# Two products instead of one transpose: x's transpose updated level by level in the RWKV recurrence of a long fused kernel

## What is computed

```python
def step(s, inp):
    r_t, w_t, k_t, v_t, a_t, b_t = inp
    sa = jnp.einsum('bhvk,bhk->bhv', s, a_t)
    s = s * w_t[:, :, None, :] + sa[..., :, None] * b_t[:, :, None, :] + v_t[..., :, None] * k_t[:, :, None, :]
    return s, jnp.einsum('bhvk,bhk->bhv', s, r_t)
...
for d, (rev, s0) in enumerate(((False, s0_f), (True, s0_b))):
    ...
    y, s = wkv_scan(s0, r, decay, kd, v, -kk, kk * a, rev)
    y_sum = y_sum + y
```

## Time and profile before

| | us |
|---|---|
| median of 3 runs | 2635.47 (2632.21 to 2637.56) |
| the profiled execution, its time | 2638.92 |
| its span in the trace | 2637.1 |
| busy in the span: TensorE, VectorE, ScalarE, GpSimd | 2322.0, 1605.5, 1076.4, 661.7 |
| the recurrence, first to last TensorE record | 1380.8 to 1813.1 |

### The profile page before, as it was taken

One profiled execution on the slowest core, in us unless ns is written; L12 is line 12 of the kernel. 1 busy time (PEld: TensorE's weight loads), 2 busy tenths in 40 slices (PEclk: granted clock), 3 DMA queues, 4 the chain that ended last, 5 costly groups with the idle time before them and its releaser, 6 DMA issues. The chain is left out here.

```text
span 2637.1 us, 50916 instructions
## 1 busy us (share of the span) xinstructions
PE 2322.0 (88%) x21292; PEld 1828.3 (69%) x21292; DVE 1605.5 (61%) x1953; ACT 1076.4 (41%) x1833; POOL 661.7 (25%) x659
## 2 busy tenths in 40 slices
PE   5998988799989579999768999999982999999993
PEld 3876755468868468888527778887661888888883
DVE  5981559541124455566484444443657999999994
ACT  3112541321014410000245655554240877777773
POOL 1221668113310023222015655550000000000000
PEclk8998999999999689999679999998995999999997
DMA  6332014511113445211161111103233999999994
GB/s 234 112 112 66 1 57 130 159 59 48 52 67 145 146 154 196 75 41 33 39 217 39 28 28 28 28 20 123 76 145 119 389 407 395 395 403 398 394 380 157
DMA packets 136488, 401.83 MB, mean 152 GB/s; under 512 B 56314, under 2 KB 67834, under 8 KB 108754
## 3 DMA queue, kind: packets, MB, share of 16 engines
q1 hardware_dynamic: 124180, 360.02, 36.8%
q0 software_dynamic: 4608, 16.78, 2.6%
q10 hardware_dynamic: 7488, 21.99, 2.2%
HBM read 341.05 MB, written 57.69 MB: 151 GB/s over the span
## 5 line engine op out<-in xcount | busy, mean ns | idle before, releaser
L3895 DVE TENSOR_TENSOR ex_wl<-ew_raw,ex_wh 128x2048 fp32r<-128x2048 f32 x192 | 435.6, 2290 | 42.2 <-ACT ex_wh L3857 38.1
L3857 ACT ACTIVATE ex_wh<-ew_raw 128x2048 fp32r<-128x2048 f32 x192 | 367.6, 1920 | 108.4 <-PE ex_U L3801 40.3
L118 PE MATMUL sp_acc<-b2h_hi,sp_wh 128*128 128x512 f32 (+1 forms) x528 | 194.9, 369 | 16.8 <-POOL sp_wl L1729 16.8
L118 PE MATMUL sp_acc<-b2h_lo,sp_wh 128*128 128x512 f32 (+1 forms) x528 | 194.7, 369 | 0.0
L118 PE MATMUL sp_acc<-b2h_hi,sp_wl 128*128 128x512 f32 (+1 forms) x528 | 194.4, 368 | 0.0
L3778 POOL DMA_INDIRECT x<-ex_o,ex_at x16 | 26.5, 1657 | 494.6 <-DVE ex_o L3918 494.6
L2512 DVE COPY_PREDICATED rc_x<-b_level,rc_chain 128x256 f32<-128x256 uint32 x160 | 64.1, 444 | 132.2 <-PE rc_chain L2600 131.6
L1727 POOL CAST sp_wh<-sp_w 128x1024 fp32r<-128x1024 f32 x26 | 28.9, 1111 | 402.5 <-DMA sp_w<-in_w_conv 226.5
L118 PEld LDWEIGHTS sp_acc<-b2h_hi,sp_wh 128*128 128x128 f32 x528 | 100.2, 190 | 34.6 <-POOL sp_wl L1729 17.2
L118 PEld LDWEIGHTS sp_acc<-b2h_hi,sp_wl 128*128 128x128 f32 x528 | 100.1, 190 | 16.6
L118 PEld LDWEIGHTS sp_acc<-b2h_lo,sp_wh 128*128 128x128 f32 x528 | 100.2, 190 | 16.3
(11 more groups left out here) (520 smaller groups left out, 5986.7 us busy)
## 6 DMA issues: line engine op xcount, KB each, us to landing
ew_raw<-in_exp_gate SPq DMA_DIRECT2D x64, 1024.0 KB, 7.5
ew_raw<-in_exp_up SPq DMA_DIRECT2D x64, 1024.0 KB, 9.3
ew_raw<-in_exp_down SPq DMA_DIRECT2D x64, 1024.0 KB, 7.9
b2p_pT<-in_ada_w SPq DMA_DIRECT2D x32, 512.0 KB, 6.0
rc_ac<-ac SPq DMA_DIRECT2D x40, 256.0 KB, 3.7
b_pj<-in_ada_w SPq DMA_DIRECT2D x8, 1024.0 KB, 12.1
ssm_wm<-in_w_merge SPq DMA_DIRECT2D x16, 512.0 KB
ac<-rp_ac SPq DMA_DIRECT2D x4, 2048.0 KB, 7.1
```

Source lines behind the costliest of these rows:

```text
L118: ins = nc.tensor.matmul(out, w[a][:, k, :], h[b][:, k, cols], start=(first and n == 0), stop=(last and n == 2))
L3857: nc.scalar.activation(wh[:, n % RING], raw[:, n % RING], ACT.Copy).then_inc(q["w_hi"], 1)
L3895: V.tensor_tensor(wl[:, n % RING], raw[:, n % RING], wh[:, n % RING].bitcast(f32), ALU.subtract).then_inc(q["w_lo"], 1)
```

## The change

From the second level on x is no longer transposed. `turned_x` for a level l of 1 to 4 now computes, with `staying`, the transposed update t1 against xt of the level before, and a new step `turned` on VectorE copies the new blocks into xt by COPY_PREDICATED, as `inverse` did already behind the last level. The first level's transpose and its copy on ScalarE stay. `factored` of levels 1 to 4 now also waits until the new product has read the old t1. The orders of TensorE, ScalarE, VectorE and GpSimd are written anew.

```diff
@@ ScalarE
 def factored(c, d, l):
     if runs(c):
         act.wait_ge(q[d]["t1_done"], LEVELS * c + l + 1)
+        if l:
+            act.wait_ge(joint["xt_done"], LEVELS * c + l + 1)
         A.activation(paired(t[d]["t1"][:]), chained(d), ACT.Copy, scale=-1.0).then_inc(q[d]["t1_ready"], 1)
...
 def v_rows(c, d, e):
...
         act.wait_ge(joint["v_done"], c + 1)
+        if c:
+            act.wait_ge(joint["s_done"], c)
+        if c > CTX_CK:
+            act.wait_ge(joint["y_crossed"], c - CTX_CK)
@@ ScalarE's order
-                    transposed(k - 2, 1, 1)
-                    transposed(k - 2, 0, 1)
...
@@ VectorE
+def turned(c, d, l):
+    if runs(c):
+        b, s = t[d], q[d]
+        dve.wait_ge(joint["xt_done"], LEVELS * c + l + 1)
+        dve.wait_ge(s["xp_done"], (LEVELS - 1) * c + l)
+        V.copy_predicated(b["xt"][:, c % 2], spread(T.level[1 - d][l][:].bitcast(u32), 1, HP), part(Z, d)).then_inc(s["xt_next"], 1)
@@ TensorE
 def turned_x(c, l):
...
         else:
-            each("x_next", (LEVELS - 1) * c + l)
+            each("t1_ready", LEVELS * c + l)
             each("xt_next", LEVELS * c + l)
-        for d in range(2):
-            last = turned(part(Z, d), t[d]["x"][:, c % 2])
+        if l == 0:
+            for d in range(2):
+                last = turned(part(Z, d), t[d]["x"][:, c % 2])
+        else:
+            last = staying(Z, lambda b: b["t1"], lambda b: b["xt"][:, c % 2])
         last.then_inc(joint["xt_done"], 1)
@@ TensorE's order
-                    advanced(k - 2, 1, 3)
...
+                    chained_x(k - 1, 0, 1)
+                    key_rows(k - 1, 0)
+                    advanced(k - 1, 1, 1)
+                    advanced(k - 1, 0, 1)
+                    turned_x(k - 1, 2)
```

More of the change, by code:

```diff
@@ L2323, in _ @@
                 k_scaled(0, 0, 0)
-                for k in range(NCK + 3):
+                for k in range(NCK + 4):
+                    k_raw(k - 2, 1)
+                    k_scaled(k - 2, 1)
+                    r_scaled(k - 2, 1)
+                    a_scaled(k - 2, 1)
+                    b_scaled(k - 2, 1)
+                    k_bias(k - 1, 0)
+                    k_scaled(k - 2, 0)
+                    k_raw(k - 1, 0)
+                    state(k - 4, 1)
+                    v_staged(k - 2, 1)
+                    state(k - 4, 0)
+                    k_gain(k, 0)
+                    v_staged(k - 2, 0)
+                    k_gain(k - 1, 1)
+                    b_raw(k - 1, 0)
+                    b_scaled(k - 1, 0)
+                    a_scaled(k - 1, 0)
+                    r_scaled(k - 1, 0)
                     k_bias(k - 1, 1)
[L2326 to L2329, removed]
                     b_raw(k - 1, 1)
[L2331 to L2344, removed]
             @block.scalar
@@ L2421, in _ @@
                 act.wait_ge(cleared, 4)
[L2422 to L2436, removed]
-                    transposed(k - 2, 1, 1)
-                    transposed(k - 2, 0, 1)
[L2439 to L2451, removed]
-                    v_rows(k - 2, 1, 1)
[L2453 to L2460, removed]
+                for k in range(NCK + 2):
+                    v_rows(k - 2, 0, 0)
+                    factored(k - 2, 1, 4)
+                    factored(k - 2, 0, 4)
+                    kept(k - 1, 1)
+                    v_rows(k - 2, 0, 1)
+                    v_rows(k - 2, 1, 1)
                     right_side(k - 2, 0)
@@ L2463, in _ @@
                     decay_out(k, 1)
-                    kept(k - 1, 1)
+                    right_side(k - 2, 1)
+                    transposed(k - 1, 1, 0)
+                    factored(k - 1, 1, 0)
+                    transposed(k - 1, 0, 0)
+                    factored(k - 1, 0, 0)
+                    kept(k - 1, 0)
+                    solved(k - 2, 1, 1)
+                    solved(k - 2, 0, 0)
+                    factored(k - 1, 1, 1)
+                    factored(k - 1, 0, 1)
+                    solved(k - 2, 1, 0)
+                    decay_in(k, 0)
+                    key_rows(k - 1, 1, 0)
+                    decay_in(k, 1)
+                    solved(k - 2, 0, 1)
+                    key_rows(k - 1, 0, 0)
+                    filled(k, 0)
+                    factored(k - 1, 1, 2)
+                    factored(k - 1, 0, 2)
+                    key_rows(k - 1, 1, 1)
+                    key_rows(k - 1, 0, 1)
+                    factored(k - 1, 0, 3)
+                    factored(k - 1, 1, 3)
+                    v_rows(k - 1, 1, 0)
+                    filled(k, 1)
             @block.vector
@@ L2561, in _ @@
                 for k in range(NCK + 2):
[L2562 to L2571, removed]
                     advanced(k - 1, 1, 3)
                     advanced(k - 1, 0, 3)
+                    summed(k - 2, 1)
+                    summed(k - 2, 0)
+                    turned(k - 1, 0, 4)
+                    turned(k - 1, 1, 4)
                     first(k, 1)
@@ L2579, in _ @@
                     masked(k, 0)
+                    right_side(k - 1, 0)
                     right_side(k - 1, 1)
-                    right_side(k - 1, 0)
                     advanced(k, 1, 0)
+                    outputs_of_state(k - 1, 1)
                     advanced(k, 0, 0)
+                    outputs_of_state(k - 1, 0)
+                    turned(k, 0, 1)
+                    turned(k, 1, 1)
+                    advanced(k, 1, 1)
+                    advanced(k, 0, 1)
+                    turned(k, 1, 2)
+                    turned(k, 0, 2)
+                    advanced(k, 1, 2)
+                    advanced(k, 0, 2)
+                    outputs(k - 1, 0)
+                    outputs(k - 1, 1)
+                    turned(k, 0, 3)
+                    turned(k, 1, 3)
                     if 4 <= k < 8:
@@ new lines, in _ @@
+                    advanced(k - 1, 1, 2)
+                    advanced(k - 1, 0, 2)
+                    outputs(k - 2)
+                    turned_x(k - 1, 3)
+                    chained_x(k - 1, 1, 3)
+                    chained_x(k - 1, 0, 3)
+                    v_rows(k - 1)
+                    advanced(k - 1, 1, 3)
+                    advanced(k - 1, 0, 3)
+                    state(k - 2)
+                    turned_x(k - 1, 4)
+                    chained_x(k - 1, 1, 4)
+                    chained_x(k - 1, 0, 4)
@@ new lines, in _ @@
+                    firsts(k)
+                    lower(k, 1)
+                    inverted(k - 1)
+                    lower(k, 0)
+                    right_side(k - 1)
+                    right_side_of_state(k - 1)
+                    turned_x(k, 0)
+                    chained_x(k, 1, 0)
+                    chained_x(k, 0, 0)
+                    solved(k - 1)
+                    advanced(k, 1, 0)
+                    outputs_of_state(k - 1)
+                    advanced(k, 0, 0)
+                    turned_x(k, 1)
@@ L2799, in rwkv_output @@
+                    chained_x(k, 1, 1)
 def rwkv_output(nc, T, I, pT, y, bonus_dram, bonus, bx_dram, xmid, mod_dram, split, ow, ow_loaded, xm, row):
```

18 lines of the change are left out of this document (1 added, 17 removed).

## The result

The changed kernel takes 2685.29 us (median of 3 runs, 2682.7 to 2692.8), for 2635.47 before: a ratio of 1.0195, 95% interval 1.0179 to 1.021. It is 50 us slower; 2624 was forecast, and the time lies outside the range. The profiled execution took 2692.8 us, 53.9 more than that of before. The recurrence, from its first to its last TensorE record, grew from 432.0 to 486.0 us (start to start): all of the loss lies there.

The account below looks back on a forecast made before the run. TensorE, 92 to 96% busy, was taken to bound the recurrence. Output chunks -4.2, context chunks -3.4 and the end chunks -4 gave -11.6 on 2638.92, 2627.3; the median lying 3.4 lower, 2624 us, range 2607 to 2646.

Parts of the forecast that it names:

- Step 3: Output chunks: interruptions by late instructions cost 0.65 us each, bounds 0 to 1.6; 21.15 per chunk, -4.2 over 14.
- the walk: One pass through the new order of a chunk with timeline prices; it left waits of 0.5 us.
- R2: Late instructions grow: every output chunk loses 1.6 us or more, 2637, or 2643 at 2.0; chance 0.12.
- R3: No interruption: all output chunks take 20.5 us, 2615 in total; chance 0.14.
- Step 1: TensorE's own work per chunk: four transpose groups out, four products in, fewer shape changes; +0.91 us, overlap giving back 0.15.
- Step 2: TensorE's waits per output chunk fall from 1.56 to 0.5 us, since xt is ready from the level's beginning.
- R1: The waits stay, being those of other borders than xt's; no gain at the ends, about 2650 us; chance 0.17.
- R4: Gain in waits and added work cancel, within 5 us of 2635; chance 0.12.
- Steps 4 and 5: Context chunks fall to 19.0 us, -3.4 over four; first and last chunk, with shorter level chains, -2 each, -4.

Follow-up runs that it names:

- e_four: Changed kernel, each new product made of 4 products of 256 columns instead of 16 of 64, part of the computation left out: 2630.79 us, ratio 0.999.
- e_eight: Changed kernel, each new product made of 8 products of 128 columns instead of 16 of 64, part of the computation left out: 2644.56 us, ratio 1.0044.
- e_before_wide: Kernel before, its three two-quarter products per chunk made of 8 products of 128 columns instead of 16 of 64, computation incomplete: 2625.64 us, ratio 0.9968.
- e_lean: Kernel before without TensorE's recurrence waits that an earlier wait of its queue covers: 2626.12 us, ratio 0.9973; once more, 2623.79.
- e_lean_after: Changed kernel without TensorE's recurrence waits that an earlier wait of its queue covers: 2657.98 us, ratio 1.0088.
- e_old_order: Kernel before with the new product and `turned`, in the old orders of all engines: 2705.83 us, ratio 1.0269.

## Why the prediction was wrong, point by point

**Step 3, "What the walk cannot see", failed.** It took the interruptions as "0.65, about as before" per output chunk, within 0 to 1.6, and as nothing for context chunks. "issue" rose by 41.7 us over 18 chunks, 2.3 per chunk, to 2.6 in each context chunk and 2.7 in each output chunk. One of the forecast's own signs of being wrong, "issue" gaps of over 1 us once per chunk, came: 20 in 18 chunks. Before, "issue" was 6.2 / 14 = 0.44 per output chunk, where the forecast had taken 0.73 from two means. The mechanism was seen, late instructions behind a dense stretch, and the forecast set it as rival R2 with 0.12; only the size of its price was off (2637 to 2643 for the 2685 measured), and the bound with it. I took the two worst interruptions of before for the worst case. They were single ones; after the change they come every one or two blocks. The rows held a hint of a wider bound: a packet every 192.60 / 44 = 4.4 us. A chunk of 1440 records and its waits, 5.7 blocks or more, then needs 25 us if fetches come no faster, and the measured chunk takes 24.49. That the 4.4 was near a limit, and not only what that kernel asked for, the rows could not tell; the changed kernel's packets come every 4.17 us in the median. As a share of a rate, the change's 1.18 times as many instructions had no room, where I read them as 1.18 times a small loss.

The Trainium skill (Runtime: NRT & Kernel Launch, "Instruction fetch mechanics") has the block of 256, and the trace agrees: 29164 instructions in 114 packets. That crossing into a block is mostly hidden, R3's case, the trace contradicts: 47.9 us of pauses.

**Step 1, TensorE's own work, held.** Forecast +0.76 per chunk. The rest in the table rose by 24.9 us. Of this 12.6 - 2.5 = 10.1 belong to the pauses, which are longer between starts than their idle time, and 2.9 to the low clock. That leaves 11.9, 0.66 per chunk. `e_four`, with nearly the same work, has +6.4; less 1.4 for its pauses (3.9 - 2.5), and with the 0.08 us that its product is shorter, four times per chunk, 5.8, it gives 10.8, 0.60 per chunk. VectorE's +3.5 per chunk came as said (10.0 to 13.6).

**Step 2, the waits, held in kind.** Waits fell by 13.8 us, 0.77 per chunk, for a forecast of 1.06. None for `rc_xt` is left, `rc_t` costs 0.20 once per chunk. R1 is refuted. With steps 1 and 2 as measured the change would have been worth 11.9 - 13.8 = -1.9 us in these chunks without late instructions, a draw, as R4 had it; `e_four` comes nearest to that, 0.999.

**Steps 4 and 5** fell with step 3: context chunks take 22.40 for the forecast 19.0, and the stage outside the 18 chunks 486.0 - 432.4 = 53.6 us for 52.4 before, where -4 was forecast. `e_four`, with a quarter of the pauses' time, has 19.05 and 427.4 - 378.1 = 49.3; its shorter product is 0.3 per chunk of that.

**The cause.** That the number of instructions does it is shown by `e_eight` and `e_four` at nearly equal array time and equal waits, and by `e_before_wide` in the other kernel; that a wait is one of these instructions, by `e_lean` and `e_lean_after`; that pauses end 2.2 to 2.9 us behind a packet, by all 56 of them. That DMA loads do it is refuted but for a fifth. What stays open is what starts a fetch: the packet that ends a pause starts 3.5 to 5.7 us behind the one ahead of it (median 4.3), while TensorE stands still for want of it, and order and waits move "issue" at an equal or nearly equal number (`e_old_order` 22.2, after 47.9).

## What to carry to other kernels

- Where many small products bound a stage, count TensorE's instructions (weight loads and waits too) against the packets of the instruction queue: near one block of 256 per 4 us, added products cost by their number, on top of the array time that they need, and here more than the waits that they took away.
- "issue" gaps within a group whose data are there, at regular counts of records, are the sign; look for them before trading a wait for more products.
- Waits that an earlier wait of the same queue covers can be left out: -0.3 to -0.4% here, and -1% in the kernel that is short of instructions.

## What the runs showed that I had not expected

- A packet of instructions ends TensorE's pause 2.2 to 2.9 us after its start, and the next starts 3.37 us later at the soonest, 4.17 in the median of the changed kernel (3.92 in `e_lean_after`).
- A wait ahead of each product makes a 32-record group over four quarters 2.41 us long for 0.63, and one over two quarters 2.22 for 1.08.
- Loads of 8.92 MB in 400 us stretch the mean distance of fetches from 4.04 to 4.26 us.
- Behind two of the longer pauses (2.16 and 1.69 us) the granted clock was 0.50 for 3.41 us, while TensorE already worked again; behind others nearly as long (1.76, 1.68) it stayed at 1.00.
